# Loading a value cache in two transfers, of 112 and 15 partitions, instead of one of 127

## The chip, the cores and the metric

The kernel runs on one core of a Trainium2 chip. The metric is the device time of one execution in microseconds (us). The engines that matter here are TensorE (PE in the profile, matrix products; PEld is its loading of weights), VectorE (DVE), ScalarE (ACT), GpSimd (POOL) and SyncE (SP); SyncE and GpSimd issue the transfers (DMAs), which 16 DMA engines carry out.

## The reference

One layer of a decoder is computed for 256 prompt tokens, 16 meta tokens ahead of them and 8 sequences with one new token each: a SwiGLU FFN at half weight, then two branches side by side (gated linear attention, GLA, and attention over a window of 128 positions) that are gated and summed, then a second FFN. The change is in the window attention of the 8 new tokens. Its values are the last 127 rows of a cache and one new row; they are used in the attention and also returned as a new cache:

```python
def swa_sample(q, k, v, meta_k, meta_v, win_k, win_v, sinks):
    ...
    kw = jnp.concatenate([win_k.astype(F32), k...], axis=1)
    vw = jnp.concatenate([win_v.astype(F32), v...], axis=1)
    ...
    p = sink_softmax(jnp.concatenate([s_meta, s_win], axis=-1), sinks)
    o = (jnp.einsum('bkgqs,bskd->bqkgd', p[..., :N_META], mv)
         + jnp.einsum('bkgqs,bskd->bqkgd', p[..., N_META:], vw))
    new_k = kw[:, -WB:].astype(win_k.dtype)
    new_v = vw[:, -WB:].astype(win_v.dtype)
```

## The kernel before

Every engine runs a program of its own, written out by hand; semaphores order them. Weights stream through the chip in slabs of 128 output columns: SyncE loads a slab (1024 KB) into one of the two buffers of `raw`, ScalarE makes its high part `w_hi` (line 617), VectorE the rest `w_lo` (line 945), and TensorE multiplies both with the tokens (lines 1344, 1345 and 1350: 48 matmuls for each slab). So TensorE computes 404 slabs one after the other, and the attention work is put between them.

The place of the change is the first eight slabs of the gate, which the code counts as `e` = 0 to 7 on all engines. In them the window attention of the 8 new tokens runs beside the slabs: at `e` = 3 TensorE computes scores against the key window (lines 1515 and 1516, after `knew_done`: the key cache is in and ScalarE has put the new key column beside it at line 779), at `e` = 4 to 6 comes the softmax, and at `e` = 7 TensorE first runs `turn(pe, 0)`, the transposes of values and keys for the first GLA chunk (lines 370 and 376), and then the weighting of the values (lines 1535 and 1536) from `v_win` and the meta values `v_meta_s`.

For `turn`, line 370 needs `vbuf`, a copy of values that GpSimd makes (line 548), and line 376 needs `kd`, a product of VectorE (`decayed_keys`, line 306). Both are in a queue behind other work. On GpSimd, the copy stands behind the whole movement of the caches, in this order: the key cache (line 533), a table for the scan (534), the value cache into 127 partitions of `v_win` (535), eight transfers of 1 KB that put the new value rows into its last partition (537), a wait for the new key column, the store of the key window (539), a wait for all nine value loads on `vwin_loaded`, the store of the value window (541), a wait for both stores (`win_out`), the load of the meta values (544), a wait for the scan of VectorE (line 1142, `prep_dve`), and the copy. On VectorE, line 306 waits for both stores too, since its result goes elsewhere into memory that is used again. A DMA adds 16 to its semaphore when it has landed, so the nine value loads are waited for as 16 x 9.

At `e` = 7 TensorE also waits for ScalarE's copies of the softmax weights (lines 794 and 795, `swa_act`) ahead of `turn`.

Of the kernel before, what the change touches and what calls it, by code (L numbers as in the profile page):

```python
# [34 lines left out]
NP_, NS, NM = 256, 8, 16  # L35
# [8 lines left out]
NH, HD, WIN = 16, 64, 128  # L44
# [21 lines left out]
def build_layer(nc, t):  # L66
    ctx = ExitStack()
    with ctx:
# [3 lines left out]
        def sem(name):  # L72
            return ctx.enter_context(nc.semaphore(name))
# [75 lines left out]
        v_win = proj[:, SK:SK + NS, 0:256]  # L149
# [13 lines left out]
        def halves(tiles):  # L163
# [40 lines left out]
        kwin_loaded, vwin_loaded, vmeta_loaded, knew_done, qpad_done = (  # L204
            sem(n) for n in ("kwin_loaded", "vwin_loaded", "vmeta_loaded", "knew_done", "qpad_done"))
# [157 lines left out]
        def turn(pe, u):  # L363

            n = CP if later(u, 0) else CK
            pe.wait_ge(g_vbuf, u + 1)
            if later(u, 0):
                pe.wait_ge(g_vtok, 2 * u)
            for j in range(8):
                last = pe.transpose(bank[4 + j // 4][0:n, (j % 4) * P:(j % 4 + 1) * P], vbuf[:, j, 0:n], ident[:])  # L370
            last.then_inc(g_vt, 1)
            pe.wait_ge(g_kd, u + 1)
            if later(u, 0):
                pe.wait_ge(g_ktok, u)
            for h in range(GH):
                last = pe.transpose(bank[3][0:n, h * DK:(h + 1) * DK], kd[:, h, 0:n], ident[:])
            last.then_inc(g_kt, 1)
# [118 lines left out]
        def _(pool):  # L496
# [35 lines left out]
            pool.wait_ge(so_done, 8)  # L532
            pool.dma_start(kT_win[:, :, :, 0:WIN], t["kT_cache"]).then_inc(kwin_loaded, 16)
            pool.dma_start(scan_keep, t["c_scan"]).then_inc(scan_loaded, 16)
            pool.dma_start(v_win[0:WIN - 1], t["v_cache"]).then_inc(vwin_loaded, 16)
            for b in range(NS):
                pool.dma_start(v_win[WIN - 1:WIN, b, :], v_new[b:b + 1, :]).then_inc(vwin_loaded, 16)
            pool.wait_ge(knew_done, 2)
            pool.dma_start(t["winkT"], kT_win[:, :, :, 1:WIN + 1]).then_inc(win_out, 16)
            pool.wait_ge(vwin_loaded, 16 * (1 + NS))  # L540
            pool.dma_start(t["winv"], v_win).then_inc(win_out, 16)
            pool.wait_ge(win_out, 32)
            pool.wait_ge(swa_pe, 1)
# [791 lines left out]
        def _(pe):  # L1335
# [19 lines left out]
            def slab(half, b, kt, x, T, ready=None, first=False, beside=None):  # L1355
                if not first:
                    pe.wait_ge(bank_free, 2 * half + b - 1)
                product(bank[b][:, 0:T], b, range(kt), x, T, 2 * half + b, ready, beside).then_inc(slab_done, 1)
# [100 lines left out]
            def turn_scores(u):  # L1459
                nk = WIN * (u % 2 + 1)  # L1460
                pe.wait_ge(p_ready, 6 * u + 6)
                if u:
                    pe.wait_ge(solo_done, 2 * u)
                for j in range(4):
                    pe.transpose(bank[5][0:NM, j * P:(j + 1) * P], sc[:, u % 2, j, nk:nk + NM], ident[:])
                for kc in range(u % 2 + 1):
                    for j in range(4):
                        last = pe.transpose(bank[6 + kc][:, j * P:(j + 1) * P], sc[:, u % 2, j, kc * P:(kc + 1) * P], ident[:])
                last.then_inc(ptr_done, 1)

            def weigh_values(u):
                g = u // 2
                cols = slice(g * HD, (g + 1) * HD)
                pe.wait_ge(pT_done, 3 * u + 3)
                out = bank[6][0:HD, :]
                pe.matmul(out, v_meta[:, cols], pT_meta, start=True, stop=False)  # L1476
                for kc in range(u % 2 + 1):
                    last = pe.matmul(out, v_tok[:, kc, cols], pT[:, kc], start=False, stop=(kc == u % 2))  # L1478
                last.then_inc(so_done, 1)
# [16 lines left out]
            for e in range(8):  # L1496
                slab(GATE_A + e // 2, e % 2, KD, x, TR)
                if e == 0:
                    turn_scores(7)
                if e == 1:  # L1500
                    weigh_values(7)
                if e == 2:
                    pe.wait_ge(solo_done, 16)
                    pe.wait_ge(pT_done, 24)
                    pe.wait_ge(gadT_done, 1)
                    for h in range(GH):
                        last = pe.matmul(bank[4 + h][:, 0:TA], a_up[0:RANK, h * DK:(h + 1) * DK], gadT[0:RANK], start=True, stop=True)
                    last.then_inc(z_done, 1)
                if e == 3:
                    pe.wait_ge(knew_done, 2)  # L1510
                    pe.wait_ge(qpad_done, 5)
                    for b in range(NS):
                        for g in range(2):
                            cols = slice(b * NH + 8 * g, b * NH + 8 * g + 8)
                            pe.matmul(bank[2][:, cols], kT_win[:, b, g, 1:WIN + 1], q_pad[:, b, 8 * g:8 * g + 8], start=True, stop=True)
                            last = pe.matmul(bank[3][0:NM, cols], kT_meta[:, g, b, :], q_pad[:, b, 8 * g:8 * g + 8], start=True, stop=True)
                    last.then_inc(swa_pe, 1)
                if e == 4:
                    pe.wait_ge(swa_act, 2)
                    pe.wait_ge(prep_dve, 4)  # L1520
                    pe.transpose(bank[4][:, 0:P], sT, ident[:])
                    pe.transpose(bank[4][:, P:P + NM], sT_meta, ident[0:NM, 0:NM]).then_inc(swa_pe, 1)
                if e == 6:
                    pe.wait_ge(swa_dve, 8)
                    pe.transpose(bank[3][:, 0:P], ssc[:, 0:P], ident[:])
                    pe.transpose(bank[3][0:NM, P:2 * P], ssc[:, P:P + NM], ident[:]).then_inc(swa_pe, 1)
                if e == 7:
                    pe.wait_ge(swa_act, 6)
                    turn(pe, 0)
                    pe.wait_ge(vwin_loaded, 16 * (1 + NS))  # L1530
                    pe.wait_ge(vmeta_loaded, 16)
                    for b in range(NS):
                        for g in range(2):
                            cols = slice(b * NH + 8 * g, b * NH + 8 * g + 8)
                            pe.matmul(bank[2][:, cols], v_win[:, b, g * P:(g + 1) * P], pTs[:, cols], start=True, stop=False)
                            last = pe.matmul(bank[2][:, cols], v_meta_s[:, b, g * P:(g + 1) * P], pTs_meta[:, cols], start=False, stop=True)
                    last.then_inc(swa_pe, 1)
# [198 lines left out]
```

## Time and profile before

| what | us |
|---|---|
| median of 3 runs (2531.07 to 2532.32) | 2531.64 |
| the profiled execution | 2533.49 |
| its span in the profile | 2531.7 |
| PE busy | 2449.3 (97%) |
| DVE busy | 1359.9 (54%) |
| ACT busy | 989.6 (39%) |
| POOL busy | 165.2 (7%) |

The profile is of one execution. Starts are counted from the start of its span. A busy time is the time in which an engine had an instruction in work; issuing a transfer is not counted as busy, but stands in the timeline and in the chain of waits. Of the chain that ended last, PE has 90% and "issue", in which an engine waited for nothing that the profile shows, 5%. A granted clock of 1.00 for TensorE is its full 2.4 GHz, 0.50 the lower level of 1.2 GHz. The DMA share of a stretch is the mean busy share of the 16 DMA engines.

### The profile page before, as it was taken

To read this page: it belongs to the slowest core of one execution; us is meant where nothing else is said; L and a number is where in the kernel's file an instruction comes from. 1 tells how busy PE (TensorE), PEld (TensorE's weight loads), DVE (VectorE), ACT (ScalarE), POOL (GpSimd) and SP (SyncE) were. 2 spreads that over 40 slices of the span, in tenths; PEclk is the share of its full clock that TensorE was granted. 3 is DMA by queue.
4 is the path that set the end of the run, shared out by engine and by line. 5 is a ranking of instruction groups with operands and counts; after the bars stand their busy time and mean duration, and the time that the engine had idled before them with its cause. 6 is when DMAs were issued, how large, how long until landed. Compare 5 with 4: busy or idle time off the path is not lost.

```text
span 2531.7 us, 47166 instructions
## 1 busy us (share of the span) xinstructions
PE 2449.3 (97%) x19106; PEld 2382.9 (94%) x19106; DVE 1359.9 (54%) x1555; ACT 989.6 (39%) x1037; POOL 165.2 (7%) x181
## 2 busy tenths in 40 slices
PE   8999999999999999975999999999999999999997
PEld 8999999999999998865888898999999999999997
DVE  6555554554556445532566455565555555555554
ACT  5333333333334344442454553344333333333332
POOL 0000000000005000011000021021000000000015
PEclk9999999999999999986898899999999999999998
DMA  5445445445445443342212354554445445545544
GB/s 207 168 158 189 166 158 184 173 154 179 174 163 168 172 149 117 122 130 69 71 66 83 139 203 152 181 178 172 181 169 196 177 163 192 181 168 197 179 166 137
DMA packets 70901, 401.78 MB, mean 159 GB/s; under 512 B 12498, under 2 KB 15218, under 8 KB 35488
## 3 DMA queue, kind: packets, MB, share of 16 engines
q1 hardware_dynamic: 62960, 386.86, 43.4%
q0 software_dynamic: 7872, 13.94, 2.0%
q8 instruction: 51, 0.84, 0.1%
q14 instruction: 18, 0.15, 0.0%
HBM read 391.43 MB, written 9.27 MB: 158 GB/s over the span
## 4 chain that ended last, share of the span: by engine, by line
PE 90%; issue 5%; DVE 2%; POOL 1%; ACT 1%; DMA 0%; DVEq 0%; SPq 0%; POOLq 0%; ACTq 0%
PE bank L1344 28%; PE bank L1350 28%; PE bank L1345 27%; PE bank L386 1%; PE bank L425 1%; PE bank L407 1%; ACT w_hi L617 1%; DVE w_lo L945 1%; PE bank L1478 0%; PE bank L423 0%; PE bank L370 0%; POOL scratch L595 0%; PE bank L1585 0%; DMA out_winv<-proj 0%; PE bank L1476 0%
## 5 line engine op out<-in xcount | busy, mean ns | idle before, releaser
L617 ACT ACTIVATE w_hi<-raw 128x2048 fp32r<-128x2048 f32 (+1 forms) x404 | 705.4, 1746 | 1234.2 <-PE bank L1350 1189.0
L945 DVE TENSOR_TENSOR w_lo<-raw,w_hi 128x2048 fp32r<-128x2048 f32 (+1 forms) x404 | 844.6, 2091 | 467.0 <-ACT w_hi L617 467.0
L1344 PE MATMUL bank<-x_hi,w_hi 128*128 128x264 f32 (+1 forms) x3440 | 896.7, 294 | 1.1 <-DVE x_lo L1288 1.1
L1345 PE MATMUL bank<-x_lo,w_hi 128*128 128x264 f32 (+1 forms) x3440 | 880.3, 289 | 0.0
L1344 PEld LDWEIGHTS bank<-x_hi,w_hi 128*128 128x128 f32 x3440 | 652.3, 190 | 21.2 <-issue 15.5
L1345 PEld LDWEIGHTS bank<-x_lo,w_hi 128*128 128x128 f32 x3440 | 652.1, 190 | 0.1
L1344 PE MATMUL bank<-y_hi,w_hi 128*128 128x264 f32 (+1 forms) x2368 | 598.2, 288 | 6.1 <-DVE y_lo L1247 5.7
L1345 PE MATMUL bank<-y_lo,w_hi 128*128 128x264 f32 (+1 forms) x2368 | 596.6, 287 | 0.0
L1350 PE MATMUL bank<-x_hi,w_lo 128*128 128x264 f32 (+1 forms) x3440 | 491.9, 293 | 0.0
L1350 PEld LDWEIGHTS bank<-x_hi,w_lo 128*128 128x128 f32 x3440 | 455.6, 191 | 4.0 <-issue 2.3
L1344 PEld LDWEIGHTS bank<-y_hi,w_hi 128*128 128x128 f32 x2368 | 447.2, 189 | 7.5 <-DVE y_lo L1247 6.9
L1345 PEld LDWEIGHTS bank<-y_lo,w_hi 128*128 128x128 f32 x2368 | 447.8, 189 | 0.0
L1350 PE MATMUL bank<-y_hi,w_lo 128*128 128x264 f32 (+1 forms) x2368 | 322.5, 286 | 0.0
L1350 PEld LDWEIGHTS bank<-y_hi,w_lo 128*128 128x128 f32 x2368 | 303.2, 189 | 0.0
L1004 DVE SCALAR_TENSOR_TENSOR hT<-bank,hT 128x280 f32 (+3 forms) x128 | 56.4, 440 | 117.5 <-PE bank L1350 117.1
L977 DVE TENSOR_TENSOR scratch<-bank,rstd 128x280 f32<-128x280 f32 (+1 forms) x88 | 38.8, 440 | 129.4 <-PE bank L1350 129.4
L501 POOL MEMSET scratch<- 128x280 f32 x3 | 1.0, 333 | 1588.5 <-DVE scratch L977 1468.8
L971 DVE TENSOR_TENSOR scratch<-bank,rstd 128x280 f32<-128x280 f32 (+1 forms) x88 | 38.8, 440 | 117.7 <-PE bank L1350 117.6
L507 POOL TENSOR_TENSOR scratch<-scratch 128x264 f32<-128x264 f32 (+1 forms) x48 | 72.4, 1509 | 3.8
L370 PE MATMUL bank<-ident,vbuf 128*32 128x128 f32 (+1 forms) x72 | 11.1, 305 | 43.1 <-POOL vbuf L548 43.1
L370 PEld LDWEIGHTS bank<-ident,vbuf 128*32 128x32 f32 (+1 forms) x72 | 6.8, 104 | 44.9 <-issue 43.3
L1040 DVE SCALAR_TENSOR_TENSOR proj<-bank,rstd 128x280 f32<-128x280 f32 (+1 forms) x28 | 12.4, 442 | 59.5 <-PE bank L1350 59.4
(254 smaller groups left out, 1284.1 us busy)
## 6 DMA issues: line engine op xcount, KB each, us to landing
raw<-in_w_in SPq DMA_DIRECT2D x176, 1024.0 KB, 4.8
raw<-in_w_out SPq DMA_DIRECT2D x128, 704.0 KB, 4.0
raw<-in_w_proj SPq DMA_DIRECT2D x52, 1024.0 KB, 4.8
raw<-in_w_merge SPq DMA_DIRECT2D x32, 1024.0 KB, 4.8
raw<-in_w_o SPq DMA_DIRECT2D x16, 1024.0 KB, 4.8
scratch<-in_state_in POOLq DMA_DIRECT2D x8, 512.0 KB, 4.0
out_state_s<-scratch POOLq DMA_DIRECT2D x8, 512.0 KB, 5.6
hT<-in_xT SPq DMA_DIRECT2D x4, 560.0 KB, 7.3
```

What stands on the lines that cost most here:

```text
L386: last = pe.matmul(cols, band[:, CP - 1 - m:2 * CP - 1 - m], Pd[:, s], start=(s == 0), stop=(half == 0 and s == CK - 1))
L407: last = pe.matmul(bank[6 + h // 2][:, (h % 2) * DV:(h % 2 + 1) * DV], k_tok[0:n, h * DK:(h + 1) * DK], gv_tok[0:n, h * DV:(h + 1) * DV], ...
L425: last = pe.matmul(out, gv_tok[:, j * P:(j + 1) * P], halves(attT)[:, :, h], start=False, stop=True)
L507: pool.tensor_tensor(acc[:, 0:T], acc[:, 0:T], sq[:, 0:T], ALU.add).then_inc(acc_done, 1)
L617: act.activation(w_hi[:, b, 0:kt * P], raw[:, b, 0:kt * P], ACT.Copy).then_inc(hi_split, 1)
L945: dve.tensor_tensor(w_lo[:, b, 0:kt * P], raw[:, b, 0:kt * P], w_hi[:, b, 0:kt * P].bitcast(F32), ALU.subtract).then_inc(lo_split, 1)
L971: dve.tensor_tensor(a_n[:, 0:T], bank[own][:, 0:T], rstd[:, 0:T], ALU.mult).then_inc(bank_free, 1)
L977: dve.tensor_tensor(b_n[:, 0:T], bank[own + 1][:, 0:T], rstd[:, 0:T], ALU.mult).then_inc(bank_free, 1)
L1004: dve.scalar_tensor_tensor(hT[:, m, 0:T], bank[b][:, 0:T], 0.5, hT[:, m, 0:T], ALU.mult, ALU.add).then_inc(bank_free, 1)
L1344: pe.matmul(out, w, x[0][:, k, 0:T], start=(k == ks[0]), stop=False)
L1345: pe.matmul(out, w, x[1][:, k, 0:T], start=False, stop=False)
L1350: last = pe.matmul(out, w_lo[:, b, k * P:(k + 1) * P], x[0][:, k, 0:T], start=False, stop=(k == ks[-1]))
```

## The change

The load of the value cache is written as two transfers of the same bytes into the same places: rows 0 to 111 into partitions 0 to 111, and rows 112 to 126 into partitions 112 to 126. Both are issued by GpSimd, one behind the other, and both count on `vwin_loaded`; the two waits on it (GpSimd's ahead of the store, TensorE's at `e` = 7) count one transfer more.

```diff
             pool.dma_start(scan_keep, t["c_scan"]).then_inc(scan_loaded, 16)
-            pool.dma_start(v_win[0:WIN - 1], t["v_cache"]).then_inc(vwin_loaded, 16)
+            pool.dma_start(v_win[0:WIN - 16], t["v_cache"][0:WIN - 16]).then_inc(vwin_loaded, 16)
+            pool.dma_start(v_win[WIN - 16:WIN - 1], t["v_cache"][WIN - 16:]).then_inc(vwin_loaded, 16)
             for b in range(NS):
                 pool.dma_start(v_win[WIN - 1:WIN, b, :], v_new[b:b + 1, :]).then_inc(vwin_loaded, 16)
             pool.wait_ge(knew_done, 2)
             pool.dma_start(t["winkT"], kT_win[:, :, :, 1:WIN + 1]).then_inc(win_out, 16)
-            pool.wait_ge(vwin_loaded, 16 * (1 + NS))
+            pool.wait_ge(vwin_loaded, 16 * (2 + NS))
             pool.dma_start(t["winv"], v_win).then_inc(win_out, 16)
...
-                    pe.wait_ge(vwin_loaded, 16 * (1 + NS))
+                    pe.wait_ge(vwin_loaded, 16 * (2 + NS))
                     pe.wait_ge(vmeta_loaded, 16)
```

In GpSimd's queue of instructions before, from the key cache to the copy into `vbuf` (`proj` is the memory of `v_win`, `scratch` that of the other tiles; behind an operation stands the tile, its source and the shape):

```order
L533 DMA scratch<-in_kT_cache 128x16x128
L534 DMA scratch<-in_c_scan 128x280
L535 DMA proj<-in_v_cache 127x8x256
L537 DMA proj<-scratch 1x16x16 x8
L539 DMA out_winkT<-scratch 2048x1x128
L541 DMA out_winv<-proj 1024x1x256
L544 DMA scratch<-in_v_meta 16x2048
L548 COPY vbuf<-proj 128x8x16
```

The same stretch of GpSimd's queue in the changed kernel, whose lines behind the new one are counted one higher:

```order
L533 DMA scratch<-in_kT_cache 128x16x128
L534 DMA scratch<-in_c_scan 128x280
L535 DMA proj<-in_v_cache 112x8x256
L536 DMA proj<-in_v_cache 15x8x256
L538 DMA proj<-scratch 1x16x16 x8
L540 DMA out_winkT<-scratch 2048x1x128
L542 DMA out_winv<-proj 1024x1x256
L545 DMA scratch<-in_v_meta 16x2048
L549 COPY vbuf<-proj 128x8x16
```

One instruction has become two; nothing else has changed its place, here or on the other engines.

## Rows read from the trace of the kernel before

**Rows 1.** Waits of PE: line, releaser, us in total, times, longest.

```profile
PE bank L370 <- POOL vbuf L548: 43.1, 1, 43.1
```

**Rows 2.** Chain of waits, 1072 to 1165: start us, us, what.

```profile
1072.95 1.18 POOL scratch L533
...
1074.67 8.81 issue
1083.48 6.72 POOL proj L535
1090.20 1.46 POOL proj L537 x3
1091.66 60.43 issue
1152.09 2.39 POOL proj L537 x5
...
1155.83 8.03 DMA out_winv<-proj
...
1164.64 0.31 POOL vbuf L548
```

**Rows 3.** Windows with POOL: stretch, length, busy (count), PE clock, DMA share, GB/s.

```profile
1074.00:1082.50 8.50, 0.67 (x2) 1.00 0.80 264
...
1130.00:1150.00 20.00, 0.00 (x0) 0.50 0.06 24
1156.00:1163.50 7.50, 0.69 (x1) 0.50 0.90 280
```

**Rows 4.** DMA issues of the span: count, KB each, median us to landing.

```profile
scratch<-in_kT_cache POOLq DMA_DIRECT2D x1, 1024.0 KB, 9.8
...
out_winv<-proj POOLq DMA_DIRECT2D x1, 1024.0 KB, 8.0
proj<-in_v_cache POOLq DMA_DIRECT2D x1, 1016.0 KB, 23.2
...
proj<-scratch POOLq DMA_DIRECT2D x8, 1.0 KB, 1.5
```

**Rows 5.** Timeline of ACT: start us, us, line, operation, tiles, forms, [idle before].

```profile
1082.75 0.23 ACT L779 ACTIVATE scratch<-scratch 128x16 f32<-128x16 f32 x1 [1.64 <-DMA scratch<-in_kT_cache]
...
1123.15 0.25 ACT L795 ACTIVATE scratch<-bank 16x128 f32<-16x128 f32 x1
```

**Rows 6.** Timeline of DVE, 1116 to 1164.

```profile
1116.27 2.63 DVE L1142 TENSOR_TENSOR_SCAN scratch<-scratch 128x280 f32<-128x280 f32 x4
...
1121.30 2.29 DVE L945 TENSOR_TENSOR w_lo<-raw,w_hi 128x2048 fp32r<-128x2048 f32 x1 [1.79 <-ACT w_hi L617]
1163.88 0.22 DVE L306 TENSOR_TENSOR a_up<-proj,hT 128x64 f32<-128x64 f32 x1 [40.29 <-DMA out_winv<-proj]
```

**Rows 7.** Timeline of PE, seven rows between 1086 and 1205.

```profile
1086.66 0.28 PE L1515 MATMUL bank<-scratch 128*128 128x8 f32 x2
...
1119.88 2.11 PE L1350 MATMUL bank<-x_hi,w_lo 128*128 128x264 f32 x16
1165.09 1.87 PE L370 MATMUL bank<-ident,vbuf 128*16 128x128 f32 x8 [43.09 <-POOL vbuf L548]
...
1167.60 0.43 PE L1535 MATMUL bank<-scratch,proj 128*128 128x8 f32 x2
...
1181.91 1.89 PE L370 MATMUL bank<-ident,vbuf 128*32 128x128 f32 x8
...
1203.97 1.05 PE L370 MATMUL bank<-ident,vbuf 128*32 128x128 f32 x8
1204.86 0.60 PE L376 MATMUL bank<-ident,a_up 128*32 128x128 f32 x4
```

**Rows 8.** Windows with line 1535: PE and PEld busy (count), PE clock, DMA share, GB/s.

```profile
1122.00:1165.00 43.00, 0.00 (x0) 0.00 (x0) 0.56 0.26 87
1167.60:1171.40 3.80, 2.37 (x12) 1.82 (x12) 0.95 0.36 91
1171.40:1181.90 10.50, 5.95 (x20) 5.00 (x20) 0.50 0.16 69
```

## The prediction

> **What bounds the kernel now.** I first read who waited for whom. One wait of TensorE stands far above the rest: the transposes of line 370 stand 43.1 us for the copy into vbuf on GpSimd, line 548 [rows 1]. The chain of waits through that place says why the copy was late: it does not pass through arithmetic at all but through GpSimd's queue of transfers [rows 2]. The reader is to see two stretches named "issue" in it, in which GpSimd stood between two transfers and no semaphore of the program held it: 8.81 us ahead of the load of the value cache (line 535), and 60.43 us after the third of the eight small transfers behind it (line 537). After the second come five more small transfers, the store of the key window, the store of the value window (8.03 us until it lands) and at last the copy at 1164.64.
>
> Why 60 us? The rates tell it [rows 3]. While the key cache (1024 KB, 128 partitions) comes in beside one weight slab, the 16 DMA engines are busy for a share of 0.80 and move 264 GB/s; while the value window (also 1024 KB, 128 partitions) is stored, 0.90 and 280 GB/s. In the stretch in which GpSimd stands, from 1130 to 1150, the share is 0.06 and the rate 24 GB/s: 0.06 is one sixteenth. One DMA engine of sixteen carries the 127-partition load, and 1016 KB at 24 GB/s are 43 us even without company. The landing time of 23.2 us shown for this load [rows 4] doesn't measure it: it counts on one semaphore with the eight small transfers. The rate is to be trusted.
>
> The Trainium skill, page "DMA: Bandwidth & Descriptors", section "Why a DMA increments its semaphore by 16 and not by 1", gives a rule for this: as many engines, 16 at most, as divide the leading dimension, so one for 127, and by it 16 for 112 and 15 for 15. The same section tells of transfers from GpSimd that are dealt over all 16 engines whatever the count, 127 among its cases; the share of 0.06 [rows 3] speaks for the divisor and against that exception here.
>
> **The change part by part.** It takes one transfer away and puts two in its place, on the same engine at the same place; both waits on the semaphore count one transfer more. Nothing else moves.
>
> *The load of 112 partitions, 896 KB.* No row shows 112 partitions. Bounds: it is carried like the 128-partition transfers, 8.0 to 9.8 us to landing [rows 4], or like the 127-partition one, 112/127 of the 60.4 us = 53.3 us. I take the first, since 112 is seven whole sets of sixteen, as 128 is eight, and the two 128-partition megabytes are the nearest rows. Its issue costs between 1.18 us (key cache) and 6.72 us (the load now) [rows 2]; I take 1.2.
>
> *The load of 15 partitions, 120 KB.* Between the 1.5 us that is the median landing of the small transfers of line 537 [rows 4] and, on one engine at 24 GB/s, 120 KB / 24 GB/s = 5 us. It hardly matters which. Issue between 0.48 us (a small transfer: 1.46 for three [rows 2]) and 1.2; I take 0.6.
>
> *The two standstills.* GpSimd went on at 1083.48, just after the key cache had landed (1072.95 + 9.8 = 1082.75), and again at 1152.09, after the value cache had. So something that holds work ahead of the DMA engines was too full for the next transfer; a load on one engine would fill one engine's share sixteen times as much as a spread one. I expect both standstills to go. If the first stays (8.81 us), the sum below doesn't change, as the slack shows.
>
> *When GpSimd is now ready.* Without standstills: 1074.67 + 1.2 + 0.6 + 8 x 0.48 = 1080.3. Then it waits for the last key column, written by ScalarE at line 779, which ends at 1082.98 [rows 5], stores the key window (1.2 us), and waits for the value loads, which land by 1076 + 9.8 + 5 = 1091 at the latest. The store of the value window goes out then and lands 8 to 10 us later, about 1101. With the old first standstill and the old issue cost: 1083.48 + 6.72 + 0.6 + 8 x 0.48 + 1.2 = 1095.8, loads in by 1105, the store in by 1114. Either way before 1118.9, when the scan of line 1142 ends on VectorE [rows 6], for which the copy into vbuf waits as well. So the copy (0.31 us) would end at 1119.3, and not at 1164.95.
>
> *What is late next.* TensorE ends its slab at 1121.99 (1119.88 + 2.11) [rows 7]. Ahead of the transposes it also waits for ScalarE's copy of line 795, which ends at 1123.40 [rows 5]; this becomes the last wait. With the 0.14 us that lie between the copy's end and the transposes now (1164.95 to 1165.09), they start at 1123.54: **41.55 us earlier**. The second set of transposes (line 376) needs the product of line 306 on VectorE, which was held by the same store (40.29 us [rows 6]); it can now follow the split that ends at 1123.59, and ends at 1123.81, before TensorE comes to it at about 1124.4. The meta values (line 544) are long there. Cover for all of this is GpSimd's slack of 5 to 18 us before 1118.9; each us by which GpSimd passes 1123.4 costs one us.
>
> *TensorE's clock.* Within the 43 us of idling the granted clock fell to 1.2 GHz, half of full (mean 0.56 [rows 8]), so the transposes ran slow: 2.51 us from 1165.09 to 1167.60. The same two lines at full clock take 1203.97 to 1204.86 + 0.60 = 1.49 us [rows 7]. **Gain 1.0.** The 64 small matmuls that follow took 14.31 us (1167.60 to 1181.91 [rows 7]): 12 of line 1535 with their partners in 3.80 us at a granted 0.95, 20 in 10.50 us at 0.50 [rows 8], so 0.63 and 1.05 us for each two. All slow would be 16 x 1.05 = 16.8, all fast 10.1. The stage now begins slow, is fast for its first quarter and slow again; after the change it begins at full clock, behind a pause of 1.5 us and the same small transposes, and may fall earlier. I take 15.3. **Loss 1.0**, with ends of -4.2 and +2.5.
>
> *Behind it* nothing new is late: the vector and scalar work of the next slabs hangs on TensorE's matmuls at the same distance as before, and weights are two buffers ahead.
>
> **Sum:** -41.55 - 1.0 + 1.0 = -41.6 us. Against the profiled execution: 2533.49 - 41.6 = 2491.9 (span 2531.7 - 41.6 = 2490.1). It lies 1.85 us above the median of the three runs, 2531.64; against that median, **2490.0 us**.
>
> One cost inside this forecast belongs in its range: the two loads now run beside the key cache, for whose column TensorE waits at line 1515. That column was ready at 1082.98, TensorE came at 1086.66 [rows 5, 7]: 3.7 us of slack. If the key cache landed later by as much as a whole 9.8 us, 6.1 us would be lost there, 2496. I take zero as likeliest, because the key cache is ahead in the same queue.
>
> **The rivals.**
> 1. *The 112 partitions still go through one engine, but all small transfers now fit.* For it: nothing before shows 112. Against: both 128-partition megabytes ran at more than ten times 24 GB/s [rows 3]. The transfer shortens from 60.4 to 53.3 us, and the 8.81 us ahead may go: 7 to 16 us less, 2516 to 2525, say 2520.
> 2. *The change does not do what it says: the pair is carried as the one was, in the same time.* Then the slow stretch has another cause than the partition count, and all stays: 2531.6. The Trainium skill, same page, section "Rules for kernel authors", has a rule that would make it so: two transfers to disjoint parts of the partitions aren't worth it, since both are dealt over the same 16 engines. By that rule the time is rival 2's; its premise, that the whole is already spread, is what the 0.06 contradicts.
> 3. *Slower: two transfers on one engine, each of which must find the queue empty.* As the 127-partition load stood 8.81 us until what was ahead had landed, the 15-partition load would stand until the 112 are in. The bytes take as long as before, and to them comes a second issue (0.6 to 6.7 us) and a landing that nothing overlaps (about 1.5 us): 2 to 8 us more in TensorE's stand, about 2536. It decides as soon as 112 partitions aren't spread and the queue takes in only one such load.
>
> **How the numbers follow.** Forecast 0.87, rival 1 0.05, rival 2 0.05, rival 3 0.03. The measurement can tell about 0.2%, 5 us, from no change. Faster by more: 0.92; within: 0.05; slower: 0.03. The range covers the forecast with its own bounds: below, the small matmuls all at full clock and a little more (2490.0 - 1.0 - 4.2 = 2485); above, the key cache late (2496) with a us for the clock, 2497.
>
> **What would show each step.** In the trace after: the load of 112 partitions at a share near that of the key cache and no stretch of 0.06; no "issue" of tens of us in GpSimd's row; the copy into vbuf right behind the scan; TensorE's wait at the transposes near 1.5 us and ended by ScalarE; the granted clock at 1.00 at their start. Wrong would be: a stretch of 24 GB/s that lasts (rival 1), GpSimd standing ahead of the second load (rival 3), a new wait of TensorE at line 1515 for the key column, or small matmuls well outside 10 to 17 us.

## The result and the profile after

The changed kernel takes 2495.72 us (median of 4 runs, 2493.6 to 2496.77); the kernel before 2531.36 (median of 4 runs, the three of the table of before and one more, 2526.91 to 2532.32). The ratio is 0.9863 with a 95% interval of 0.9847 to 0.9878: 35.6 us less. The time lies in the predicted range (2485 to 2497), 5.7 us above the predicted 2490.0. The profiled execution took 2494.72 us, with a span of 2492.9.

TensorE's waits after the change (line, releaser, us in total, times, longest); the changed kernel counts lines behind 535 one higher:

```profile
PE bank L1376 <- ACT w_hi L618: 10.0, 1, 10.0
PE bank L1345 <- DVE y_lo L1248: 5.6, 3, 3.3
...
PE bank L370 <- ACT scratch L796: 1.5, 1, 1.5
```

The 43.1 us of [rows 1] are 1.5, and what ends them is now ScalarE's copy of the softmax weights. GpSimd's timeline (start us, us, line, operation, tiles, [idle before and what ended it]) shows why:

```profile
1072.23 1.18 POOL L533 DMA_DIRECT2D scratch<-in_kT_cache  x1 [7.85 <-PE bank L1479]
1073.40 0.55 POOL L534 DMA_DIRECT2D scratch<-in_c_scan  x1
1073.94 0.85 POOL L535 DMA_DIRECT2D proj<-in_v_cache  x1
1074.79 0.61 POOL L536 DMA_DIRECT2D proj<-in_v_cache  x1
1075.40 3.85 POOL L538 DMA_DIRECT2D proj<-scratch  x8
1083.06 1.17 POOL L540 DMA_DIRECT2D out_winkT<-scratch  x1 [3.81 <-ACT scratch L780]
1089.65 0.87 POOL L542 DMA_DIRECT2D out_winv<-proj  x1 [5.41 <-DMA proj<-scratch]
1097.52 0.51 POOL L545 DMA_DIRECT2D scratch<-in_v_meta  x1 [7.00 <-DMA out_winv<-proj]
1120.02 0.34 POOL L549 COPY vbuf<-proj 128x128 f32<-128x128 f32 x1 [21.99 <-DVE scratch L1143]
```

Both standstills of [rows 2] are gone. The two loads are issued in 0.85 and 0.61 us, where the one took 6.72; all value loads are in by 1089.65, 15.7 us after the first issue; and GpSimd, which was the last, now itself stands 22 us for the scan of VectorE. The window rows (busy, clock, DMA share, GB/s) that answer to [rows 3] show no stretch at 0.06 any more (a share a little over 1.00 counts packets that began in the stretch and ended behind it):

```profile
1074.00:1086.00 12.00, 6.42 (x11) 0.86 1.01 280
1086.00:1096.00 10.00, 0.87 (x1) 0.77 1.00 356
```

### The profile page after: what moved, and what is told of

The parts are those of the page before. It is cut to its first block, busy times and chain, and to the rows that moved or that the text cites. A ratio compares the mean times of both kernels' runs of the same rounds, so it can differ in the third digit from the quotient of the medians.

```text
span 2492.9 us, 47167 instructions
## 1 busy us (share of the span) xinstructions
PE 2452.3 (98%) x19106; PEld 2385.9 (96%) x19106; DVE 1360.8 (55%) x1555; ACT 989.3 (40%) x1037; POOL 162.2 (7%) x182
## 4 chain that ended last, share of the span: by engine, by line
PE 93%; DVE 2%; issue 2%; ACT 1%; POOL 1%; DMA 0%; DVEq 0%; SPq 0%; ACTq 0%; POOLq 0%
PE bank L1345 29%; PE bank L1351 29%; PE bank L1346 28%; PE bank L386 1%; PE bank L407 1%; PE bank L425 1%; ACT w_hi L618 1%; DVE w_lo L946 1%; PE bank L1479 0%; PE bank L423 0%; PE bank L370 0%; POOL scratch L596 0%; PE bank L1586 0%; PE bank L1477 0%; PE bank L1537 0%
## 5 line engine op out<-in xcount | busy, mean ns | idle before, releaser
L386 PEld LDWEIGHTS bank<-scratch,band 128*32 128x32 f32 x512 | 38.6, 135 | 4.1 <-issue 1.7
L386 PE MATMUL bank<-scratch,band 128*32 128x64 f32 x512 | 41.4, 255 | 1.1 <-DVE scratch L343 1.1
```

The source lines that it names most:

```text
L386: last = pe.matmul(cols, band[:, CP - 1 - m:2 * CP - 1 - m], Pd[:, s], start=(s == 0), stop=(half == 0 and s == CK - 1))
```

## The experiments

Two questions were open: what makes the load slow (the partition count, the number of transfers, their size, or the queue that GpSimd fills), and why the gain was smaller than forecast.

**113 and 14 partitions.** As many transfers as in the change, the larger one by one partition bigger and prime:

```diff
-            pool.dma_start(v_win[0:WIN - 16], t["v_cache"][0:WIN - 16]).then_inc(vwin_loaded, 16)
-            pool.dma_start(v_win[WIN - 16:WIN - 1], t["v_cache"][WIN - 16:]).then_inc(vwin_loaded, 16)
+            pool.dma_start(v_win[0:113], t["v_cache"][0:113]).then_inc(vwin_loaded, 16)
+            pool.dma_start(v_win[113:WIN - 1], t["v_cache"][113:]).then_inc(vwin_loaded, 16)
```

> The load of the value cache in two transfers of 113 and 14 partitions. Theory (the number of DMA engines is the largest up to 16 that divides the count of partitions; 113 is prime): the first goes through one engine at 24 GB/s, 904 KB are 38 us alone and 113/127 of 60.4 = 54 us beside other work; TensorE still stands 17 to 36 us at line 370, time 2505 to 2525. Rival (splitting as such, or a shorter first transfer, is what helps): spread, no stand, 2493 to 2497.

Measured: 2525.67 us, ratio 0.9975 (0.9962 to 0.9988) to 2531.65 before. GpSimd's timeline of this kernel:

```profile
1080.08 6.05 POOL L535 DMA_DIRECT2D proj<-in_v_cache  x1 [8.22 <-issue]
1086.13 0.61 POOL L536 DMA_DIRECT2D proj<-in_v_cache  x1
1086.72 3.89 POOL L538 DMA_DIRECT2D proj<-scratch  x8
1144.39 1.17 POOL L540 DMA_DIRECT2D out_winkT<-scratch  x1 [53.78 <-issue]
```

One partition more in the first transfer, and most of the gain is gone: the first standstill is there again, and the long one has only moved behind the eight small transfers. TensorE stood 34.1 us, as the theory expected; the time is 0.7 us above its range. So it isn't the splitting.

**126 and 1.** The same edit with 126 in place of 113; 126 is no multiple of 16, but 14 divides it.

> Two transfers of 126 and 1 partitions. Theory (a divisor, 14 for 126): 14 engines with 9 partitions each, the load is in some 2 to 3 us later than with 112, which the idle time of GpSimd hides: 2493 to 2497. Rival (only whole sets of 16 partitions are spread): 126 partitions on one engine, a stretch of 24 GB/s, TensorE stands over 30 us, 2515 to 2531.

Measured: 2493.7 us, ratio 0.9855 (0.9839 to 0.9872). The store of the value window, which waits for all value loads, went out at 1089.81, as early as with 112 partitions (1089.65), and TensorE stood 1.5 us. The 2 to 3 us that the load was to come later don't show. Whole sets of 16 aren't needed; 126 does as well.

**96 and 31.** The same edit with 96.

> Two transfers of 96 and 31 partitions. 31 is prime: by the theory 248 KB go through one engine, 248 KB / 24 GB/s = 10.3 us alone, 31/127 of 60.4 = 14.7 us beside other work. Theory (what counts is only whether the copy into vbuf is ready when the scan of VectorE ends; GpSimd stood 22 us for that scan): hidden, 2493 to 2497, GpSimd's wait for the scan 7 to 15 us shorter. Rival (one-engine loads cost their length in proportion): 10 to 15 us slower than with 112 and 15, 2505 to 2511.

Measured: 2491.36 us, ratio 0.9845 (0.9829 to 0.9862). One window and two rows of GpSimd's timeline:

```profile
1096.00:1102.00 6.00, 0.00 (x0) 0.72 0.06 25
```

```profile
1104.18 0.87 POOL L542 DMA_DIRECT2D out_winv<-proj  x1 [21.95 <-DMA proj<-scratch]
...
1117.90 0.34 POOL L549 COPY vbuf<-proj 128x128 f32<-128x128 f32 x1 [6.28 <-DVE scratch L1143]
```

A stretch at 0.06 and 25 GB/s is back: the 31 partitions come through one engine, and GpSimd waits 22 us for them instead of 5.4. It costs nothing, since the wait for the scan shrinks from 22.0 to 6.3 us. Lateness counts only beyond the scan. The way of the load, though, was not 10 to 15 us long: from its issue at 1072.70 to the store at 1104.18 are 31.5, the time behind other loads in the queue included.

**24 and 103.** The same edit with 24, to pass the scan by some us.

> Two transfers of 24 and 103 partitions, for the price of lateness; 103 is prime. Theory (one engine; time in proportion): 103/127 of 60.4 = 49 us; with nothing standing ahead of it the load lands near 1124, the store of the value window lands near 1133, the copy into vbuf ends near 1134 and TensorE stands some 12 us at line 370 instead of 1.5: 2500 to 2506. If the standstill of 8 us ahead of the load stays, as it did with 113: 2508 to 2514. Rival (a load that is late at all costs all of it): 2520 and more.

Measured: 2515.29 us, ratio 0.9931 (0.9911 to 0.9951), outside the expected 2500 to 2506. Its timeline:

```profile
1072.71 5.54 POOL L536 DMA_DIRECT2D proj<-in_v_cache  x1
...
1137.22 0.87 POOL L542 DMA_DIRECT2D out_winv<-proj  x1 [53.90 <-DMA proj<-scratch]
```

The standstill ahead of the load is gone, as expected, but from the issue to the store it took 64.5 us, not 49. The rate shows where the time went: GpSimd's queue moved 0.14 MB in the 6 us from 1102 to 1108, when no weights moved, and 0.12 MB in the 12 us from 1110 to 1122, beside 1.70 MB of weights. That is 23 GB/s alone and 10 beside slabs, which fits a load that started earlier and shared its engine with more slabs. Sizing a one-engine load in proportion to its partitions was wrong (31: 31.5 us, 103: 64.5, 127: 67.0, the last from the next experiment). What it costs once it is late was right: TensorE stood 22.4 us, 20.9 more than in the changed kernel, and the time is about 20 to 23 us above the three measurements of that.

**The small transfers first.** In the kernel before, the eight transfers of 1 KB are issued ahead of the load of 127 partitions:

```diff
-            pool.dma_start(v_win[0:WIN - 1], t["v_cache"]).then_inc(vwin_loaded, 16)
             for b in range(NS):
                 pool.dma_start(v_win[WIN - 1:WIN, b, :], v_new[b:b + 1, :]).then_inc(vwin_loaded, 16)
+            pool.dma_start(v_win[0:WIN - 1], t["v_cache"]).then_inc(vwin_loaded, 16)
```

> The kernel before with one edit: the eight small transfers are issued ahead of the load of 127 partitions. Theory (the load on one engine lands after some 60 us, and the store of the value window has to wait for it wherever GpSimd stands): GpSimd now stands behind the load, at the store of the key window or at the wait for the loads; gain only the 2 to 3 us of small transfers that stood behind it, 2527 to 2532. Rival (only the standstill in issuing hurts; the load lands after the 23.2 us that the page shows): 2491 to 2500.

Measured: 2529.94 us, ratio 0.9995 (0.9975 to 1.0015). GpSimd's timeline and the row of its DMA issue (KB, us to landing):

```profile
1073.83 3.86 POOL L536 DMA_DIRECT2D proj<-scratch  x8
1084.60 6.72 POOL L537 DMA_DIRECT2D proj<-in_v_cache  x1 [6.91 <-issue]
1151.86 1.17 POOL L539 DMA_DIRECT2D out_winkT<-scratch  x1 [60.54 <-issue]
```

```profile
proj<-in_v_cache POOLq DMA_DIRECT2D x1, 1016.0 KB, 67.0
```

The standstill is as long as before and merely stands elsewhere; and with the load the last to count on its semaphore, the landing reads 67.0 us, where [rows 4] had 23.2. The 23.2 was an effect of the shared semaphore, as the prediction held, and the changed order by itself gains nothing that can be told from noise.

**One transfer for each sequence.** Still 127 partitions, but eight transfers (TensorE's wait on `vwin_loaded` changes as GpSimd's does):

```diff
-            pool.dma_start(v_win[0:WIN - 1], t["v_cache"]).then_inc(vwin_loaded, 16)
+            for b in range(NS):
+                pool.dma_start(v_win[0:WIN - 1, b, :], t["v_cache"][:, b]).then_inc(vwin_loaded, 16)
...
-            pool.wait_ge(vwin_loaded, 16 * (1 + NS))
+            pool.wait_ge(vwin_loaded, 16 * (NS + NS))
```

> The value cache in eight transfers of 127 partitions, one for each sequence (127 KB each, one piece of 1 KB in each partition). The partition count is still prime. If each transfer goes through one engine and the next takes another engine, eight run side by side: in by about 1105 at the latest, 2491 to 2500. If all take the same engine: eight times 127 KB at 24 GB/s, 43 to 60 us, 2522 to 2536. If splitting over the partitions was what mattered: also 2522 to 2536.

Measured: 2494.15 us (two runs), ratio 0.9841 (0.9819 to 0.9864). The time is that of eight transfers side by side, but the reason is another. The count of small DMA packets tells it (row of 1070 to 1165 in the view of DMA; first this kernel, then in fences of their own the changed kernel and the kernel before):

```profile
DMA packets 2693, 12.93 MB, mean 136 GB/s; under 512 B 592, under 2 KB 592, under 8 KB 1648
```

```profile
DMA packets 2646, 13.21 MB, mean 139 GB/s; under 512 B 514, under 2 KB 514, under 8 KB 1568
```

```profile
DMA packets 6144, 11.24 MB, mean 118 GB/s; under 512 B 4258, under 2 KB 4258, under 8 KB 5312
```

The kernel before has 3744 small packets more than the changed one. Most of them have 16 bytes, and in the packet records of GpSimd's queue these can be counted alone: 3810 in the kernel before, 2 in the changed kernel, none with the eight transfers. The load of before is 1016 KB, carried in 254 packets of 4 KB, and 15 x 254 = 3810. They are through at 1108, some 43 us before the load itself, so they didn't stand between its own packets. The counts of the other splits come out of one rule with these: if k engines carry a transfer, each of the other 16 - k gets one 16-byte packet for every 4 KB packet that one of the k carries. The records don't name the engines; that it is these that get them is read from the counts.

| load | engines k | 16-byte packets worked out | counted |
|---|---|---|---|
| 127 (before) | 1 | 15 x 254 = 3810 | 3810 |
| 113 + 14 | 1, 14 | 15 x 226 + 2 x 2 = 3394 | 3394 |
| 24 + 103 | 12, 1 | 4 x 4 + 15 x 206 = 3106 | 3106 |
| 96 + 31 | 16, 1 | 15 x 62 = 930 | 930 |
| 126 + 1 | 14 | 2 x 18 = 36 | 36 |
| 112 + 15 (after) | 16, 15 | 1 x 2 = 2 | 2 |

In these loads k is the largest divisor of the partition count up to 16 (the single partition of 126 + 1 went in eight packets of 1 KB and added none of 16 bytes). The eight transfers of 127 partitions have none either: they are dealt over all engines. That 127 is prime didn't matter there, and the theory of the divisor fell as a rule for every transfer.

**Two transfers by sequence.** To find what distinguishes these from the load of before, which has eight separate pieces of 1 KB in each partition (edit against the kernel before; both waits count one transfer more, as in the change):

```diff
-            pool.dma_start(v_win[0:WIN - 1], t["v_cache"]).then_inc(vwin_loaded, 16)
+            for b in range(2):
+                pool.dma_start(v_win[0:WIN - 1, 4 * b:4 * b + 4, :], t["v_cache"][:, 4 * b:4 * b + 4]).then_inc(vwin_loaded, 16)
```

> The value cache in two transfers of 127 partitions, four sequences each (508 KB; 4 pieces of 1 KB in each partition instead of the 8 of before and the 1 of the transfers by sequence). If the shape decides (a partition with several pieces that lie apart goes by the divisor, a partition with one piece is dealt over all engines): one engine each, some 3800 packets under 512 bytes as in the kernel before; on one and the same engine 2522 to 2536, on two different engines 508 KB / 24 GB/s = 21 us alone and up to 40 beside other work, TensorE's stand 1.5 to 20 us, 2492 to 2515. If the size of a transfer or their number decides: spread, some 600 such packets, 2491 to 2497.

Measured: 2506.23 us (two runs), ratio 0.9908 (0.9877 to 0.994). Its DMA row and a window of its trace:

```profile
DMA packets 6278, 11.97 MB, mean 126 GB/s; under 512 B 4305, under 2 KB 4305, under 8 KB 5359
```

```profile
1101.00:1106.00 5.00, 0.00 (x0) 1.00 0.13 48
```

The small packets are back (3810 of 16 bytes, 15 for each of 254), and 48 GB/s at a share of 0.13 are two engines side by side: each transfer has one engine, and the second another than the first. TensorE stood 14.0 us. So of 127 partitions, one piece in each is dealt over all engines, four or eight pieces in each are not. The shape is the likeliest reason, but not the only one left: the spread transfers are also the smallest, 127 KB, and the smallest that went through one engine has 248 KB (31 partitions). A limit of size between the two was not tested.

The Trainium skill, page "DMA: Bandwidth & Descriptors", section "Why a DMA increments its semaphore by 16 and not by 1", has both: the divisor, and an exception for "some direct copies" from GpSimd, which go over 16 engines with an equal count of partitions for each, rounded up. Its examples for the exception are 127 partitions on all 16 and 100 on 15. It doesn't say which copies. The prediction set the exception aside, rightly for this load; the runs show both sides of it, and that the shape, or the size as said, tells which.

**The price of TensorE's stand.** With the profiles of all kernels that change only this load, the time is the stand at line 370 plus nearly the same number each time, 2489.8 to 2495.7 (stand and time are of different executions; the changed kernel alone, measured three times, spreads from 2492.4 to 2495.7):

| load | stand us | time us | time less (stand - 1.5) |
|---|---|---|---|
| 127 (before) | 43.1 | 2531.4 | 2489.8 |
| 127, small ones first | 39.6 | 2529.9 | 2491.8 |
| 113 + 14 | 34.1 | 2525.7 | 2493.1 |
| 24 + 103 | 22.4 | 2515.3 | 2494.4 |
| 2 x 127 by sequence | 14.0 | 2506.2 | 2493.7 |
| 96 + 31 | 1.5 | 2491.4 | 2491.4 |
| 126 + 1 | 1.5 | 2493.7 | 2493.7 |
| 8 x 127 by sequence | 1.5 | 2494.2 | 2494.2 |
| 112 + 15 (after) | 1.5 | 2495.7 | 2495.7 |

**The size of the gain.** The changed kernel was measured twice more, beside new runs of the kernel before.

> The changed kernel once more, for its size and for the granted clock. Both theories of the gain say the same of the time: 2493 to 2497 us. On the 2.8 us that were lost behind the small matmuls of the value window: if they belong to where the clock happens to rise again, a second profile can show the products of line 407 anywhere between 2.2 us (as before) and 3.7 us; if the earlier start itself costs them, it shows 3.7 us again and the dip at the slab ahead of line 1516 as well.

Measured: 2492.44 us against 2531.65, ratio 0.9853 (0.9836 to 0.9869). Line 407 took 3.78 us again, and the dip ahead of line 1516 was there again, at a clock of 0.54. That is what the second theory said; but the kernel with 126 and 1, whose transposes start as early, has no dip there, and the second profile of the kernel before, below, has the dip and the 3.78 us without the change.

> The changed kernel a third time, beside new runs of the kernel before, for the size of the gain: 35.6 and 39.2 us in the first two comparisons. If those differ by the run alone, a third lies between 34 and 41 us, 2491 to 2497. In its profile, the time from the first transposes of line 370 to the first matmuls of line 386 was 29.5 and 31.0 us; 29 to 34 is expected, and TensorE's wait at line 370 at 1.5 us again.

Measured: 2495.26 us against 2531.71, ratio 0.9864 (0.9841 to 0.9887). So the gain is 35.6, 39.2 and 36.4 us in three comparisons. And the kernel before once more, for a second profile:

> The kernel before once more, for a second profile of the time from the first transposes of line 370 to the first attention matmuls of line 386, at the granted clock. In the first profile that took 27.7 us, with the clock at its full level for 3.4 us of it, and 29.5 to 31.0 us in four changed kernels. If that is chance of where the clock rises and falls, this profile can show 27.7 to 31; if the change costs it, 27.7 again. Time 2527 to 2534.

Measured: 2535.36 us in one run. From the first transposes of line 370 to the first attention matmuls of line 386, in order before, before again, after, again and third (stretch, length, PE busy and count, granted clock, DMA share, GB/s):

```profile
1165.09:1192.79 27.70, 27.70 (x145) 0.70 0.13 44
```

```profile
1164.28:1197.62 33.34, 33.34 (x144) 0.56 0.10 36
```

```profile
1124.51:1153.98 29.47, 29.47 (x144) 0.65 0.21 72
```

```profile
1124.19:1155.14 30.95, 30.95 (x144) 0.61 0.20 69
```

```profile
1124.79:1154.27 29.48, 29.48 (x145) 0.65 0.20 72
```

The same work takes 27.7 or 33.3 us in the unchanged kernel, by the clock that was granted: 0.70 or 0.56. Both the 33.3 us and the time lie above what was expected. The profile on which the prediction was worked out was the favourable one. In a change of 36 us this alone is an uncertainty of several us. Over the profiles of all kernels so far and the next one, the stretch takes 27.7 to 33.3 us in the six with a stand of 14 us or more, 30.0 in the mean, and 29.5 to 31.0 in the seven with 1.5 us or none, 30.1 in the mean. So the change doesn't show in the stretch as a whole. Line 407 alone differs: 3.78 us in all seven, 2.2 to 2.4 in four of the six.

**Taking away the last wait.** ScalarE copies the softmax weights, and VectorE makes the product for line 376, ahead of their next splits:

```diff
             for e in range(8):
                 half, b = GATE_A + e // 2, e % 2
+                if e == 6:
+                    act.wait_ge(swa_pe, 3)
+                    act.activation(pTs, bank[3][:, 0:P], ACT.Copy).then_inc(swa_act, 1)
+                    act.activation(pTs_meta, bank[3][0:NM, P:2 * P], ACT.Copy).then_inc(swa_act, 1)
                 split_hi(half + 1, b, KD)
...
                 dve.tensor_tensor(siga[:, m], bank[b][:, 0:TR], rstd[:, 0:TR], ALU.mult).then_inc(bank_free, 1)
+                if between is not None:
+                    between()
                 split_lo(half + 1, b, KD)
```

Here `between` is, for `e` = 6 only, the wait for both stores and the two products that stood behind the split.

> The changed kernel; what ends TensorE's last wait of 1.5 us at line 370 is done sooner: ScalarE copies the softmax weights (lines 795 and 796 of the changed kernel) ahead of its next split, and VectorE makes the product of line 306 ahead of its next split. Theory (that copy is the last wait, the product the next): 1.5 us less at line 370, 2490 to 2495, about 1.5 us under the changed kernel. Rival (another wait takes its place at once): no change.

Measured: 2489.55 us against 2533.65, ratio 0.9833 (0.9816 to 0.9851). TensorE's timeline of this kernel:

```profile
1120.55 2.11 PE L1354 MATMUL bank<-x_hi,w_lo 128*128 128x264 f32 x16
1122.50 1.03 PE L370 MATMUL bank<-ident,vbuf 128*16 128x128 f32 x8
```

The transposes follow the slab without a wait. The time is just under the expected 2490 to 2495. That the wait is gone is shown; that the time is lower than the changed kernel's by 1.5 us isn't, since the intervals overlap.

**The small matmuls beside the slab.** On top of that edit, the 64 small matmuls are issued beside the second half of the slab of `e` = 7, in place of the loop after `turn(pe, 0)`:

```diff
-                slab(GATE_A + e // 2, e % 2, KD, x, TR)
+                slab(GATE_A + e // 2, e % 2, KD, x, TR, beside=window_values if e == 7 else None)
```

`window_values` waits as the loop did and then issues one group of four matmuls ahead of each matmul with `w_lo`.

> As the kernel with the early copies, and the 64 small matmuls of the value window are issued beside the second half of the slab at e = 7, one group of four behind each matmul with w_lo, instead of in a row after the transposes. Theory (in a row they make the granted clock fall to 1.2 GHz, which costs 16 groups of 1.05 instead of 0.63 us and slows the transposes, line 407 and part of the slab behind): the clock stays at 2.4 GHz there, 6 to 10 us less than the changed kernel, 2483 to 2489. Rival (the clock falls all the same, or the matmuls with weights of their own between large ones cost as much): 0 to 3 us less.

Measured: 2488.32 us, ratio 0.982 (0.9806 to 0.9833), 1.2 us under the kernel with the early copies on the same chip; the intervals of the two overlap. The granted clock (third from the right) in three stretches:

```profile
1117.00:1123.00 6.00, 6.00 (x49) 1.00 0.40 168
1123.00:1130.00 7.00, 7.00 (x37) 0.69 0.39 152
1130.00:1140.00 10.00, 10.00 (x42) 0.50 0.00 0
```

The time lies in the range of the theory, but the clock fell all the same, so its mechanism, that one large matmul between each four small ones would keep the clock up, is refuted. What the edit itself gave is read behind all of this, at the first matmul of line 386: it starts at 1151.48, with the early copies at 1152.03, 0.55 us later, and in the three profiles of the changed kernel at 1153.98 to 1155.14. So 6 to 10 us weren't to be had this way. This version and the one with the early copies have the lowest medians of all. The interval of this one lies below all three of the changed kernel (the lowest of those begins at 0.9836), that of the early copies doesn't; how much of that is the two edits isn't shown, as they were measured on another chip than the changed kernel.

## Why the prediction was right, and where its size was off

**The bound and its cause** were read rightly from the rate of 24 GB/s at a share of 0.06: one engine of sixteen. The kernels with 113, 103 and 31 partitions and their small packets confirm it, and those with 112 and 126 its removal. The reason given for 112, seven whole sets of sixteen, was not needed: 126 is no such set. And the comparison with "more than ten times 24 GB/s" was read too high: the 264 GB/s have a weight slab in them, and the 280 both stores. 1024 KB in 8.0 to 9.8 us are 107 to 131 GB/s, which is still more than four times the 24.

**The two standstills** both went, as taken; the kernel with 113 partitions has both again, the one with 103 only the wait for the landing, the one with two transfers by sequence shorter ones of 4.4 and 34.6 us. That fits something with a limited room ahead of the DMA engines, in which a one-engine load takes up much (the 16-byte packets take room on the other fifteen too); how large it is wasn't measured directly.

**GpSimd's way** was put at ready for the key column by 1080.3; it was 1079.25 (1075.40 + 3.85). The loads were to be in by 1091 and were by 1089.65, the value window's store was to land near 1101 and was in by 1097.5. The key cache was not delayed (ScalarE's copy ended at 1082.8), so the cost put into the upper end of the range didn't come.

**What is late next** was named rightly: ScalarE's copy, 1.5 us.

**The sum** was too large by 2.8 us between the two profiled executions: 2533.49 - 41.6 = 2491.9 was forecast and 2494.72 came. Two terms hold that. TensorE's transposes start at 1124.51, and not at 1123.54, because part of the slab ahead of the scores ran at half clock this time:

```profile
1081.00:1084.70 3.70, 3.70 (x20) 0.54 1.02 243
```

(The dip cost 1.5 us in a slab that began 0.7 us earlier than before; 0.8 us are left at line 1516 and 0.97 at the transposes. The second profile of the kernel before has this dip at the same place, so it isn't owed to the change.) And from the transposes to line 386 it took 29.47 us and not 27.70, 1.77 us, which is the term of TensorE's clock. The -1.0 for the transposes came as -1.2 (1.31 us instead of 2.51; the prediction's 1.49 was counted to the end of line 376, its 2.51 to the start of what follows). The small matmuls took 14.5 us instead of 15.3. But line 407 and the beginning of the slab behind, which stood in the sum with nothing, ran at half clock and took 2.8 us more:

```profile
1142.96 3.78 PE L407 MATMUL bank<-scratch 16*128 16x256 f32 x8
1146.67 0.59 PE L1345 MATMUL bank<-x_hi,w_hi 128*128 128x264 f32 x1
```

The failing step is "Behind it nothing new is late": that was true of the waits and not of the clock. The stretch was priced from one profile of before, and as shown above this one lies at the low end of 27.7 to 33.3 us. That the measured 2495.72 still lies in the range is in part luck: the room above 2490 was meant for a late key cache, which didn't come; the clock and the difference between profiled execution and median took it. The other 3 us of the difference lie between profiled execution and median: the profile of before was 2.1 us above its median, that of after 1.0 below. Whether anything of the 36 to 39 us depends on the change beyond the stand and the clock can't be told at this spread.

**The rivals.** Rival 1 describes what 113 partitions do: one engine, all small transfers issued, 53.8 us of standstill for the 53.3 worked out, and 2525.7 us at the edge of its 2516 to 2525. Rival 3's sign didn't come even there: the 14 partitions were issued right behind the 113, in 0.61 us. Rival 2 is refuted: the 35.6 us are there. The rule of the Trainium skill that the prediction names beside it (page "DMA: Bandwidth & Descriptors", section "Rules for kernel authors": two transfers to two halves of the partitions aren't worth it, since each is spread over all 16 engines) has a premise that this load didn't meet.

## What to carry to other kernels

When a transfer is late, read the rate and the DMA share in a stretch in which nothing else moves: 24 GB/s at 0.06 was one engine of sixteen here; then look at the partition count and at how many separate pieces each partition has, and split off the odd partitions or send one piece per partition (shown here for pieces of 1 KB, 127 KB in each transfer). Then see who waits behind it on the issuing engine: here the 43 us went through a copy that had nothing to do with the value cache but stood behind it in a queue, and a one-engine load of 31 partitions was free because its lateness was covered. Before a remainder of a few us is explained by the change, look at a second profile of the unchanged kernel.

## What the runs showed of the hardware

A load of 127 partitions issued by GpSimd went through one engine when each partition had four or eight separate 1 KB pieces, and through all when it had one (127 KB in a transfer); the next such one-engine load took another engine (48 GB/s for two). Loads of 8 KB in each partition went through as many engines as the largest divisor of their partition count up to 16 (113, 103 and 31: one; 126: 14). For each 4 KB packet on the one engine there were 15 packets of 16 bytes (3810 for 254). Beside the weight slabs such a load was slower than its 24 GB/s: 10 GB/s with 103 partitions. And GpSimd needed 6.72 us to issue the load of 127 partitions, 6.05 for 113, 5.54 for 103 and 2.05 for 31, against 0.85 for 112 and 1.02 for 126.
